# Token projections of two later layers: narrow weight blocks one at a time, or two side by side in groups of four tiles

## What is computed

```python
def even_layer(x, norm, w_in, gq_a, gk_a, rpb, gq_b, gk_b, w_out, ang_row, ang_col):
    h = rmsnorm_2(x, norm)
    qa, ka, va, qb, kb, vb, gate = _split(h @ w_in, SPLIT_E)      # 3328 columns
    # q and k normalised per head, qb and kb rotated
    oa = neighbourhood_attention(qa, ka, va, rpb)
    ob = attend_blocks(qb, kb, vb, D_HEAD ** -0.5)
    return (concat(oa, ob) * silu(gate)) @ w_out

def odd_layer(x, norm, w_in, g_cq, w_cq_b, g_ckv, w_ckv_b, ...):
    h = rmsnorm_2(x, norm)
    cq, ckv, kpe, qd, kd, vd, gate = _split(h @ w_in, SPLIT_O)    # 2976 columns
    q, kv = rmsnorm_2(cq, g_cq) @ w_cq_b, rmsnorm_2(ckv, g_ckv) @ w_ckv_b
    # heads normalised, part of each rotated, lambda from lam_q1 .. lam_k2
    oc = attend_blocks(qc, kc, v_c, ...)
    od = diff_attend_blocks(qd[.., 0], qd[.., 1], kd[.., 0], kd[.., 1], vd, lam, ...)
    return (concat(oc, rmsnorm_2(od, g_sub_d) * (1 - lam_init)) * silu(gate)) @ w_out
```

## Time and profile before

| | |
|---|---|
| three runs | 3074.01, 3074.38, 3077.2 us (median 3074.38) |
| the profiled execution's own time | 3066.51 us |
| its span | 3064.8 us |
| TensorE busy, matmuls | 2911.5 us |
| VectorE, ScalarE, GpSimd busy | 1622.3, 1161.2, 1069.8 us |
| mean granted clock of TensorE | 0.986 of 2.4 GHz |
| even layer's projections and head preparation | 1412.1 to 1731.8 us |
| odd layer's, with the latents | 2176.9 to 2516.8 us |

### The profile page before, as it was taken

One profiled execution on the slowest core, in us unless ns is written; L12 is line 12 of the kernel. 1 busy time (PEld: TensorE's weight loads), 2 busy tenths in 40 slices (PEclk: granted clock), 3 DMA queues, 4 the chain that ended last, 5 costly groups with the idle time before them and its releaser, 6 DMA issues.

```text
span 3064.8 us, 47759 instructions
## 1 busy us (share of the span) xinstructions
PE 2911.5 (95%) x17540; PEld 2508.7 (82%) x17540; DVE 1622.3 (53%) x3106; ACT 1161.2 (38%) x2101; POOL 1069.8 (35%) x690
## 2 busy tenths in 40 slices
PE   7999998999999999999999999999999987789999
PEld 6689866778888888888999988997897986678887
DVE  3899838343222232313029278982212959988861
ACT  3311264242212211213124356772322635557750
POOL 2223020432222235662225433444331544332335
PEclk9999998999999999999999999999999999999999
DMA  4123331431111113442297444313335863131223
GB/s 144 60 98 126 109 78 29 138 117 49 48 48 48 48 55 91 137 164 82 93 211 227 118 109 101 83 58 125 135 138 180 239 163 72 49 76 35 72 88 129
DMA packets 219514, 319.44 MB, mean 104 GB/s; under 512 B 81286, under 2 KB 163078, under 8 KB 217174
## 3 DMA queue, kind: packets, MB, share of 16 engines
q1 hardware_dynamic: 184774, 273.10, 30.0%
q10 hardware_dynamic: 33360, 39.98, 3.8%
q0 software_dynamic: 1216, 4.20, 0.5%
HBM read 225.76 MB, written 91.47 MB: 104 GB/s over the span
## 4 chain that ended last, share of the span: by engine, by line
PE 70%; DVE 9%; issue 3%; ACT 1%; POOL 1%; SPq 0%; DMA 0%; DVEq 0%; POOLq 0%; ACTq 0%; PEldq 0%
PE psum L2575 16%; PE psum L530 15%; PE psum L2356 8%; PE psum L2778 8%; PE psum L1085 4%; PE psum L1116 4%; PE psum L1096 3%; PE psum L794 3%; DVE arena L3195 3%; PE psum L772 2%; PE psum L783 2%; DVE diff L1475 1%; PE psum L1390 1%; PE psum L1367 1%; DVE arena L3184 1%
## 5 line engine op out<-in xcount | busy, mean ns | idle before, releaser
L2575 PE MATMUL psum<-parts_ffn 128*128 128x512 f32 x2112 | 482.0, 391 | 3.8 <-DVE parts_ffn L2532 3.8
L2575 PEld LDWEIGHTS psum<-parts_ffn 128*128 128x128 f32 x2112 | 398.2, 189 | 87.2 <-issue 2.2
L530 PE MATMUL psum<-parts_even,parts_ffn 128*128 128x256 f32 x2496 | 305.0, 285 | 3.0 <-DVE parts_ffn L2919 1.8
L530 PEld LDWEIGHTS psum<-parts_even,parts_ffn 128*128 128x128 f32 x2496 | 302.8, 193 | 3.4 <-DVE parts_ffn L2919 2.0
L2645 DVE SCALAR_TENSOR_TENSOR arena<-psum,arena 128x1023 f32<-128x1023 f32 x88 | 112.9, 1283 | 328.2 <-ACT arena L2629 322.0
L530 PE MATMUL psum<-parts_odd 128*128 128x248 f32 x2304 | 270.5, 280 | 2.7 <-DVE parts_odd L2532 1.8
L530 PEld LDWEIGHTS psum<-parts_odd 128*128 128x128 f32 x2304 | 268.3, 190 | 3.8 <-DVE parts_odd L2532 2.0
L576 ACT ACTIVATE arena<-psum 128x256 f32<-128x256 f32 (+2 forms) x240 | 87.5, 375 | 392.5 <-PE psum L530 388.7
L444 PE MATMUL psum<-parts_mixer 128*128 128x512 f32 x912 | 210.2, 391 | 0.3 <-DVE parts_mixer L287 0.3
L444 PEld LDWEIGHTS psum<-parts_mixer 128*128 128x128 f32 x912 | 170.7, 188 | 35.8 <-DVE parts_mixer L287 0.5
L2102 DVE TENSOR_SCALAR_CACHE_REDUCE choose_flags<-arena,choose_bits 128x384 uint8<-128x384 f32 (+2 forms) x198 | 174.3, 942 | 1.2
(11 more groups left out here) (370 smaller groups left out, 5889.5 us busy)
## 6 DMA issues: line engine op xcount, KB each, us to landing
arena<-ffn_up_b SPq DMA_DIRECT2D x44, 512.0 KB, 3.2
arena<-ffn_down_k SPq DMA_DIRECT2D x44, 512.0 KB, 3.7
arena<-x SPq DMA_DIRECT2D x8, 2048.0 KB, 8.7
arena<-w_in_e SPq DMA_DIRECT2D x13, 1024.0 KB, 6.7
e_tokens<-arena ACTq DMA_DIRECT2D x26, 512.0 KB, 3.1
x<-arena SPq DMA_DIRECT2D x24, 512.0 KB, 3.7
arena<-w_in_o SPq DMA_DIRECT2D x12, 992.0 KB, 6.6
o_tokens<-arena ACTq DMA_DIRECT2D x24, 496.0 KB, 3.0
```

Source lines behind the costliest of these rows:

```text
L530: last = pe.matmul(self.bank(t), self.hT[:, a, k, t * P:(t + 1) * P], self.weights.parts[:, self.weights.slot(s), b, k, :], start=(k, a, b ...
L2575: last = pe.matmul(self.core.psum[:, 4 * u + 2 * s + h, :], parts[:, s, a, k, :], self.hT[:, b, k, h * HALF:(h + 1) * HALF], start=(k, a, ...
```

## The change

A new `ProjectPairs` takes the place of `ProjectTokens` in both stages of both later layers, and a new `SplitPairs` that of `SplitWeights`.

- Two weight blocks lie side by side, so that one matmul moves 512 columns (496 in the odd layer) into a full bank. Seven blocks are three pairs and a single; the last pair of the odd layer's second stage is multiplied as two singles (`last_apart`).
- The weights of a pair are loaded, split and freed in four chunks of two k-blocks each.
- Four tiles, one for each bank, are multiplied with chunk 0, then with chunk 1 and so on; then the other four tiles. A unit is now 6 matmuls.
- The first stage starts on a chunk when the low parts that it reads are out (`rows_ready`); the transposes of tiles 4 to 7 come after units 10 and 13.
- ScalarE stores two tiles at a time.
- The second stage waits for its banks one by one. In the odd layer it uses four banks and head preparation four (before two and six): transposes of groups 4 and 5 come in the middle of a step (`again=True`).
- GpSimd rotates first and then splits, whatever the lag, the chunks by a table.
- Gains, bias load, spread and read-back go into the first even stage, the mask and store behind it, lambda behind the second even stage.

```diff
+class SplitPairs:
+    CHUNKS, EACH = 4, KT // 4
...
+    def load(self, sp, p, c):
+        if p:
+            sp.wait_ge(self.low_ready, self.CHUNKS * (p - 1) + c + 1)
+        else:
+            hold(sp, self.chunk_after(c))
...
+    def split(self, pool, p, c, freed):
+        raw = self.raw_chunk(p, c)
...
+        pool.wait_ge(self.loaded[c], 16 * p + 16)
+        hold(pool, freed(p - 1, c) if p else self.parts_chunk_after(c))
+        pool.tensor_copy(high, raw).then_inc(self.high_ready, 1)
+        pool.wait_ge(self.high_ready, self.CHUNKS * p + c + 1)
+        pool.tensor_tensor(low, raw, high.bitcast(F32), ALU.subtract).then_inc(self.low_ready, 1)
+class ProjectPairs(Stage):
...
+        self.subs = [(p, 0, self.weights.slots(p)) for p in range(self.weights.passes)]
+        if last_apart:
+            p = self.subs.pop()[0]
+            self.subs += [(p, 0, 1), (p, 1, 1)]
...
+    def units(self):
+        B = len(self.banks)
+        return [(j, c, t) for j in range(self.N) for g in range(0, TT, B) for c in range(self.weights.CHUNKS) for t in range(g, g + B)]
...
+    def multiply(self, pe, j, c, t):
+        B, (p, s, n) = len(self.banks), self.subs[j]
+        if s == 0 and t == 0:
+            pe.wait_ge(self.weights.low_ready, self.weights.CHUNKS * p + c + 1)
+        if c == 0 and TT * j + t >= B:
+            pe.wait_ge(self.act_out, TT * j + t - B + 1)
+        elif c == 0 and self.banks_after is not None:
+            hold(pe, self.banks_after(t))
+        if j == 0 and self.rows_ready is not None:
+            self.wait_rows(pe, c, t)
...
+    def wait_rows(self, pe, c, t):
+        if t < 4:
+            pe.wait_ge(self.rows_ready, max(self.weights.EACH * (c + 1), t + 1))
+        elif t == 4:
+            pe.wait_ge(self.rows_ready, KT + self.weights.EACH * (c + 1))
...
 class ProjectAndPrepare(Stage):
+        self.split_at = {n: [(p, c) for p in (1, 2) for c in range(4) if 4 * p - 2 + (c + 1) // 2 == n] for n in range(self.steps)}
...
     def gpsimd(self, pool):
+        for c in range(4):
+            weights.split(pool, 0, c, project.freed)
         for n in range(self.steps):
             if n == 1:
                 prep.clear(pool)
-            if self.lag == 2 and 0 <= n - 1 < TT:
+            if 0 <= n - 1 < TT:
                 prep.rotate(pool, n - 1)
...
+            for p, c in self.split_at[n]:
+                weights.split(pool, p, c, project.freed)
...
     def tensor(self, pe):
         for n in range(self.steps):
             if 0 <= n - self.lag < TT:
                 prep.turn(pe, n - self.lag)
-            for unit in self.units(n):
+            for at, unit in enumerate(self.units[n]):
                 project.multiply(pe, *unit)
+                if at == len(self.units[n]) // 2 - 1 and prep.banks < prep.G and 0 <= n - self.lag < TT:
+                    prep.turn(pe, n - self.lag, again=True)
     def scalar(self, act):
+        for n in range(self.steps):
             if self.lag == 2 and n < TT:
                 prep.square(act, n)
             if 0 <= n - self.lag < TT:
                 prep.scalar_take_out(act, n - self.lag)
...
+            if self.lag == 3:
+                if 0 <= n - 1 < TT:
                     prep.root(act, n - 1)
+                if n < TT:
                     prep.square(act, n)
+            for j, c, t in self.units[n]:
+                if c == 3:
+                    project.take_out(act, j, t)
...
+        first.sync_pieces = {1: gains.sync, 2: spread_biases, 3: biases.read_back}
+        first.pool_pieces = {1: biases.clear}
+        add(Part(scalar=scales.exponentials, vector=scales.weigh_heads))
...
-        rest = ProjectTokens(core, "tok4b", a["w_in_o"][6:12], hT, o_tok[:, 1488:2976], 6, 248, [], [], [], banks=(6, 7),
-                             stage_place=core.words - 1984)
+        rest = ProjectPairs(core, "tok4b", a["w_in_o"][6:12], hT, o_tok[:, 1488:2976], 6, 248, [], [], [], banks=(4, 5, 6, 7),
+                            stage_place=core.words - 1984, last_apart=True)
```

283 lines of the change are left out of this document (190 added, 93 removed).

## The result

The changed kernel takes 3088.36 us (median of 6 runs, 3083.4 to 3092.03), the kernel before beside it 3074.32 us (6 runs, 3072.85 to 3078.78). The ratio is 1.0047, with an interval of 1.0037 to 1.0058: slower by half a per cent. The forecast was 3082, slower, with 3066 to 3096.

A forecast was written before the change was run, and what follows sets the result against it. TensorE bounds the even layer and odd first half, a four-engine loop through VectorE the odd second half. Terms: -19 - 5.9 - 2.1 - 3 + 39 = +9, rounded to +8 over the median 3074.38: 3082 us, range 3066 to 3096.

The forecast's parts named there:

- part 5: Odd second half: GpSimd rotates before it splits, so the last chunk waits behind the last rotation; +39 us, bounds +29 and +46.
- The clock's 2 x 3 us: Odd second half: TensorE's two long waits for weight chunks each bring the low clock, 3 us apiece.
- Rival (b): Odd second half stays Vector-bound, the last chunk being there when step 8 wants it; -20 us, 3054; chance 0.22 with milder cases.
- Rival (c): Wide matmuls save little, costing 0.238 us as columns come from two places in SBUF; 3100 us, chance 0.05.
- Part 1: Wide matmuls in the token projections: 16.5 us saved in the even layer, 5.9 in the odd first half, nothing in its second.
- the slope: Wide matmuls: cost per column, (0.2257-0.1200)/256, used to price a 496-column product at 0.2191 us.
- Part 2: First stages' projections start by weight chunk: 2.1 us gained each, and -3 us of clock in one layer, none in the other.
- Part 3: Joints of the even layer: about 2 us of waits go, 2 us given back at neighbour attention; even layer 19 us in all.
- part 4: Moved work (bias spread, read-back, mask, store, lambda, latents' load) costs 0; upper bounds 1 us for lambda, 3 us for latents.
- The term for lambda: Lambda behind even head preparation: VectorE idle there, only the Exp follows the last eviction, beside TensorE's first scores; 0, bounds 0 and +1 us.
- the forecast +8: Whole kernel: terms sum to +9 us, rounded to +8 since every wait in the odd second half is taken as exposed.

The follow-up runs named there:

- The experiment on step 8: Changed kernel with only step 8 of the odd second half splitting its weight block before rotating the last tile; 3073.2 us, 0.9992 of the kernel before.
- all splits first: Changed kernel with GpSimd splitting its weight chunks before rotating at every step of the odd second half; 3063.4 us, 0.9985 of the kernel before.
- root first: Splits-first version, with ScalarE also taking a tile's root ahead of the earlier tile's evictions in the odd second half; 3062.3 us, 0.9978 of the kernel before.
- the best kernel: Changed kernel with single blocks, old stage and order in the odd second half, pairs elsewhere; 3049.3 and 3047.4 us, 0.9923 and 0.9917 of the kernel before.

## Why the prediction was right, and where it was not

**The deciding step, part 5, held.** The sum forecast +39 us for the odd second half, and it measured +37.6, and +39.0 to +41.3 in the four versions that leave this half as changed. Both waits are the same in all five, 8.71 to 8.73 and 14.97 to 14.98 us. The last chunk's split stands behind the last rotation and the wait for it was 14.97 us (15 forecast), the one for chunk 1 8.72 us (8 forecast). From tile 6's rotation to tile 7's it took 2484.65 - 2461.32 = 23.3 us (21.9 forecast, 16.9 before). The last rotation came 9.7 us later (10 forecast, 13 with half of the clock's 6). Behind it stand 27.9 us (23, and 3 for the clock). One term was short: from tile 7's second transposes (2513.42 + 1.03) to landing at 2530.64 it is 16.2 us, against 13 forecast, since stores and loads did not shorten with the evictions. The experiment on step 8 shows the mechanism as well as the size: 17 us come back by that one swap, 14.3 in the profile. The clock's 2 x 3 us were right in sum and not in their parts: the two long waits cost 1.7 to 1.9 us each, and two short ones, of 0.67 and 2.47 us before the 24 wide products at 2399.49 and 2417.21, cost about as much (7.22 and 7.04 us for what takes 5.42 with nothing ahead). In three other executions the first of them cost nearly nothing (5.66 to 5.68 us). The prediction's reading that waits of 1.8 us leave the clock alone is right for the trace of before and is no rule.

**Rival (b), faster, decided where it was said to.** It hung on whether the last split is there before TensorE's 13th unit of step 8. Here it is not, by 15 us. But the rival's price was wrong as well: with step 8 swapped the split is there, and the kernel comes out at 0.9992, with all splits first at 0.9985, 3070 us on that scale and not 3054. It took the second half for VectorE-bound still, and with pairs TensorE's own work ahead of the last transposes sets its end (the windows above). Rival (c) was off in its sum: by its own 0.238 us the even layer misses 14.2 us and not 13.6, and its 4.5 us for the odd half follow from nothing in it.

**Part 1 had the even layer right and the odd one too high.** A 512-column product took 10.93/48 = 0.2278 us (0.2257 forecast from the earlier trace rows), so 1152 pairs saved 0.0122 x 1152 = 14 us and not 16.5. A 496-column one took 110.76/492 = 0.2251 us; the forecast took 16 columns off along the slope and had 0.2191. The 0.0103 us of each pair were 0.0043, and the odd first half's 5.9 us were 2.5. That term was mis-sized by more than a factor of two: it is a small difference of two large durations, and 3% of one of them is over half of it. By the Trainium skill (TensorE: Matmul & The Clock Gate, the section on 56 ns against 53.3 ns) a pair would save the one fixed cost of about 2.5 ns, an estimate. The rows of after disagree: they have 12.2 ns at 512 columns and 4.3 ns at 496, so neither that rule nor the slope fits both.

**Part 2 was right in size, and its split between the layers was luck.** The odd start gained 1.8 us, the even one 0.9, as its last transposes themselves ran slowly (1.94 us against 1.06 in the earlier trace rows). The clock did keep up in one layer and fall in the other, as forecast, but that belongs to the execution and not to the layer: of ten profiled executions with this start in the even layer, five kept the full clock and five fell, and of ten in the odd layer nine kept it. In this execution the odd layer's 66 products took 14.85 us, at the 0.2251 us of its steady part, the even layer's 16.90, which is 1.9 us over 66 x 0.2278. Together with the starts the odd first half gave 7.2 us by 2.5 + 1.8 + 2.9. A start at the low clock costs 3.0 us here, so over all those executions the mean is 1.8 us for both layers, where the forecast had 2.9.

**Part 3.** The even layer gave 17.9 us to the next layer's transposes, against 19. The first neighbour scores came 18.9 us earlier (1722.18, before 1732.76, less the 8.3 us), with GpSimd's split still the last to arrive. The 1.0 us between the two figures went to lambda (part 4). Over the nine executions of this code the layer gave 13.7 to 21.0 us, so 17.9 against 19 is a closer hit than one execution can show.

**Part 4 had one term wrong and misread another.** Of the bias work its 0 held: nothing waits for it. But the prediction treated that move as neutral, and the experiment makes it a condition of the even layer's gain: with the paired second stage the old place costs 17.5 us in that layer's profile and 21 to 27 us in the times, of a gain of 17 to 21. The term for lambda, "0, bounds 0 and +1", fell short. From the first neighbour score to the first transposes of its weights it was 2.94 us before (1732.76 to 1735.70) and 3.99 after (1722.18 to 1726.17), so even the won race costs the +1 of the bound, and a lost one costs 5.3. The prediction put the Exp beside TensorE's first scores and did not ask what waits behind the two VectorE steps that follow it: VectorE's first work on those scores.

**What was not forecast.** Behind the diff scores the changed kernel took 545.7 us, the kernel before 541.0. The version with only the even layer changed has 545.2 there, the one with root first 540.0 and the rest between 544.3 and 547.1, so this is no part of the odd layer's edit. It is none of the even layer's or of lambda's either: with only the odd layer changed, and the rest as before, it is 545.5. The lone short value besides root first is the one profiled execution of before, so chance is the likeliest cause, which is argued and not shown. It is half of the 9 us by which the profiled sum, +17.2, stands over the forecast +8. Most of the other half is the odd first half and its clock (7.2 for 8 + 3). The medians, at +14, lie between.

## What to carry to other kernels

When an engine serves two consumers in one loop, write down for the last trip which of its jobs stands behind which, and put the one whose inputs have long been there first: here one swapped pair of calls, 3 us of work behind a rotation that waits for a slower engine, was worth 17 us. Price an edit for each stage by what bounds that stage: wide matmuls and an earlier start gained 17 us where TensorE owned the chain, and the paired stage with its four banks cost 20 us beyond the order of the splits where VectorE did, so the best kernel uses both forms. And a move that costs nothing may be what makes another part of the same change pay; undo it by itself before calling it neutral. The other way round, a single small VectorE step moved to where GpSimd works can cost 4 us; look at which engine is first there in several profiles, not in one.

## What the runs showed of the hardware

- A product of 496 columns costs nearly what one of 512 does: 0.2251 and 0.2278 us, where two of 248 and two of 256 cost 0.2294 and 0.2400. Reading 512 columns from one run or two makes no difference (156.37 us for the same piece of the chain in both).
- The same pause does not always bring the low clock. At a start where TensorE had paused 2.99 us, run eight transposes and gone on at once, five of ten profiled executions ran the transposes in 1.06 us and the next 66 products in 15.22 to 15.25 us (granted clock 1.00), and five took 1.94 and 17.21 to 17.28 us (in the changed kernel the clock was 0.50 over the transposes and 0.55 over the next 4.8 us). Behind 2.13 us of pause nine of ten kept the full clock. Where a second pause of 1.8 to 1.9 us followed the transposes, all six starts lost 1.3 to 3.0 us.
- 24 narrow products that take 3.0 us took 4.69 and 4.95 us behind waits of 8.72 and 14.97 us. The granted clock of the changed kernel there, in two windows at those products and one behind them:

```profile
2464.00:2469.00 5.00, 4.65 (x26) 4.65 (x27) 0.00 (x0) 0.00 (x0) 3.20 (x3) 0.60 0.00 0
2487.60:2492.60 5.00, 4.93 (x26) 4.93 (x27) 0.00 (x0) 2.31 (x4) 0.02 (x1) 0.57 0.07 23
2493.00:2513.00 20.00, 20.00 (x178) 20.00 (x177) 0.00 (x0) 6.74 (x15) 0.00 (x0) 1.00 0.37 106
```

  At 0.60 and 0.57 most of the two windows ran at 1.2 GHz (0.50), and from 2493 on all was at 2.4 GHz. Each such wait cost 1.7 to 1.9 us of clock beside its own length, not the 3 us that the forecast took.
- A split slows VectorE by holding one instruction up, not by slowing all. Its normalization of a tile, 32 instructions in 6.90 us alone and 11.38 beside a whole block's split, took 7.61 and 8.81 us beside the halves. In the second case one instruction of the 32 took 2.00 us where the mean alone is 0.22. It began 0.19 us after GpSimd's subtraction (2448.10, 2.07 us) and ended 0.1 us after it. VectorE's timeline of the changed kernel, the 32, and that one in a window of its own (2448.6 to 2449.1):

```profile
2447.60 8.81 DVE L3376 SCALAR_TENSOR_TENSOR arena<-arena 128x96 f32<-128x96 f32 x32
...
2448.29 2.00 DVE L3376 SCALAR_TENSOR_TENSOR arena<-arena 128x96 f32<-128x96 f32 x1
```

  Lambda's step of 0.16 us that took 4.39 beside a subtraction of 4.50 us is the same thing.
- The first layer, which no version changes, ends up to 8 us apart in the thirteen profiled executions, so two profiles should be laid over each other at the last unchanged instruction, and not at zero.
